# A chain of small attention steps set further apart beside a stream of matmuls, and three places for a convolution's input

## The chip, the cores and the metric

The kernel runs on one core of a Trainium2 chip. The metric is the device time of the whole program in microseconds (us); below, a time is the median of a few executions, and the profile is of one execution more. The engines are TensorE (PE, matmuls; PEld are its weight loads), VectorE (DVE), ScalarE (ACT), GpSimd (POOL) and SyncE (SP, which here only issues DMAs).

## The reference, cut to what matters

A transformer block of 512 tokens by 1024 features in float32: a feed-forward part, a hybrid mixer, a second feed-forward part, and then two more layers of other kinds. Only the mixer is touched by the change. It projects the normalized input `h` to many columns, and then runs two branches:

```python
proj = h @ w_in
# attention: 3 groups of 4 heads; group g has a causal window, dilation 1, 4, 16
q_a = partial_rope(q_a); k_a = partial_rope(k_a)      # rotates the first 32 of 128 dims
o_g, lse_g = dilated_window_attention(q_g, k_g, v_g)  # softmax over a near/far band
alpha = softmax(stack(lse_g)); att = sum(alpha * o_g)
# mLSTM: 4 heads of 256
qk = silu(causal_depthwise_conv(qk_m, conv_w, conv_b))   # 4 taps over time
hm = mlstm_chunkwise(q_m, k_m, v_m, i, log_f)
ml = sigmoid(o_m) * (rmsnorm(hm) * head_g)
y = (sigmoid(g_a) * (att @ w_att) + sigmoid(g_m) * (ml @ w_ml)) @ w_out
```

Each projection is computed as three products of split operands (high times high, low times high, high times low).

## The kernel before, in words

**Tiling.** Weights come in chunks, 128 output columns by 1024 input rows each. For a chunk `i` SyncE loads `RAW`; ScalarE writes the high half `WH` (`highs`, recorded at helper line 1031, event `hi`); VectorE writes the low half `WL` (`lows`, line 1651, event `lo`); TensorE runs 8 x 3 matmuls of 128x512 in `fm` (lines 410, 411, 413; the last one is line 415) into one of two side banks of PSUM; ScalarE evicts the bank (event `ev`). There are three slots of `WH` and `WL`, so `highs(i+2)` waits for the matmuls of chunk `i-1`.

**The side steps.** The small work of the mixer rides beside this stream. Each engine's program is written out by hand by its own function (`tensor_program`, `scalar_program`, `vector_program`), and in each the same generators stand in a list `behind.work`. `behind.step()` advances every generator of the list once, in the order in which they were appended. Each chunk has four steps. TensorE steps after every second `k`, so its steps lie 6, 12, 18 and 24 matmuls into the chunk. ScalarE and VectorE do all four steps of a chunk together. In their instruction order a chunk is:

```python
def fm():                      # scalar_program; vector_program has lows(i + 2)
    highs(i + 2)
    for _ in range(plan[i][1] // 2):
        behind.step()          # 4 times
    ...                        # then ScalarE waits for the matmuls of i and evicts (ev)
```

A generator that waits for a semaphore therefore holds up everything behind it in its engine's order, the next `highs` or `lows` among it. `behind.finish()` at the end of a turn runs what is left of the list with no matmuls between. `behind.bank()` hands out PSUM banks 5 and 6 for short use; all engines' programs must ask in the same order, so the yields of one generator are matched over the engines.

**The turns.** The mixer has eight turns `n`. Turns 0 to 3 project attention head `n` in nine chunks (q, k, v of three groups; `att_project`), turns 4 to 7 project mLSTM head `n-4` in eight chunks (four of them convolution inputs, then two values, then two gates; `ml_project`). Beside turn `n` run the small steps of the head of turn `n-1`: `attention(hd)` beside turns 1 to 4, `mlstm(hd)` beside turns 5 to 7 and what follows. Each is the first in the list of its turn. Behind them in the list come the generators of the chunks themselves, each appended after its chunk: `rope_first` (q and k: ScalarE issues two DMAs in its second step, VectorE rotates with three operations in its fifth), `to_tokens` (values: TensorE transposes, lines 585 and 586, ScalarE copies back), `conv` (VectorE's four operations in its first step, ScalarE's SiLU in its fourth).

**The chain of one attention head**, in the side steps of its turn (chunk `c` of a turn holds the steps 4c-3 to 4c):

| hand-over | engine, line | step before |
|---|---|---|
| scores near and far (`s near`, `s far`) | TensorE L612, L621 | 1 |
| mask and maxima (`mx near`, `mx far`) | VectorE L1660, L2002, L2008 | 3 |
| exponentials near and far (`ex near`, `ex far`) | ScalarE | 5 |
| `spread` | VectorE L1651 (32 columns) | 7 |
| `moved` (8 small matmuls) | TensorE L631 | 8 |
| `moved read`, `part in` | VectorE L1663, L1651 | 9 |
| `part` | ScalarE | 10 |
| `parts`, then far weights scaled (`pr far`) | VectorE L1651, L1657 | 11 |
| `back` (8 small matmuls) | TensorE L644 | 12 |
| near weights scaled (`pr near`) | VectorE | 13 |
| four rounds of transposes and products | TensorE L657, L667, ScalarE | 13 to 17 |

**The convolution's input** is one tile for each parity of the turn, `SETS[:, s, 8, :]`; ScalarE's eviction of the next one waits for the convolution that read the one before.

Of the kernel before, what the change touches and what calls it, by code (L numbers as in the profile page):

```python
# [16 lines left out]
T = 512  # L17
# [286 lines left out]
def small(m, name):  # L304
    a, b = SMALL[name]
    return m["SM"][:, a:b]
# [10 lines left out]

# [42 lines left out]
def tensor_program(pe, t, m):  # L363
# [215 lines left out]

    def to_tokens(i, dst, tok):  # L580
        b = yield from behind.bank()
        w.wait_ge(*at("ev", i))
        clear(b)
        for tb in range(3):
            pe.transpose(PS[:, b, tb * P:(tb + 1) * P], dst[:, tb * P:(tb + 1) * P], ident)
        pe.transpose(PS[:, b, 3 * P:4 * P], dst[:, 3 * P:4 * P], ident).then_inc(*tick("pe", "tt", i))
        free[b] = ("tok", i)
        behind.leave(b)
        tok.append(i)
# [12 lines left out]
    def attention(hd, s, tok):  # L602
        while len(tok) < 9:
            yield
        i0 = MIX + 1 + 9 * hd
        for g in range(3):
            w.wait_ge(*at("rope", i0 + 3 * g))
            w.wait_ge(*at("rope", i0 + 3 * g + 1))
# [15 lines left out]
        free[4] = free[7] = ("sm far", hd)  # L624
        for _ in range(7):
            yield
# [7 lines left out]
        free[b] = ("moved read", hd)  # L634
        yield
        behind.leave(b)
        for _ in range(3):
            yield
# [7 lines left out]
        ins.then_inc(*tick("pe", "back", hd))  # L646
        free[b] = ("back read", hd)
        yield
        behind.leave(b)
# [23 lines left out]
    def conv(i, tok):  # L673
        for _ in range(3):
            yield
        tok.append(i)
# [346 lines left out]
def scalar_program(a, t, m):  # L1023
# [202 lines left out]

    def to_tokens(i, dst, tok):
        b = yield from behind.bank()
        w.wait_ge(*at("tt", i))
        act(dst, PS[:, b, :], ACT.Copy, "tok", i)  # L1230
        behind.leave(b)
        tok.append(i)
# [27 lines left out]
    def attention(hd, s, tok):  # L1260
        while len(tok) < 9:
            yield
        near, far = small(m, "near"), small(m, "far")
        for _ in range(4):
            yield
# [5 lines left out]
        for n in range(4):  # L1271
            pr = weighed(m, 4 + n)
            act(pr, pr, ACT.Exp, *(("ex far", hd) if n == 3 else ()), bias=far[:, n:n + 1], accum_out=far[:, 4 + n:5 + n])
        for _ in range(3):
            yield
        b = yield from behind.bank()
        yield
        behind.leave(b)
        yield
        part = small(m, "part")  # L1280
        w.wait_ge(*at("part in", hd))
        act(part, part, ACT.Exp, "part", hd)
        yield
        yield
        b = yield from behind.bank()
        yield
# [15 lines left out]
    def conv(s, i, dst, tok):  # L1302
        for _ in range(3):
            yield
        w.wait_ge(*at("conv", i))
        act(dst, dst, ACT.Silu, "silu qk", i)
        tok.append(i)

    raw_free = [None, None]

    def ml_project(hd, s, tok):
        for c in range(4):
            i, b = fm(), side_bank()
            w.wait_ge(*at("mm", i))
            set_clear(s)
            if raw_free[s] is not None:
                w.wait_ge(*at("conv", raw_free[s]))
            raw_free[s] = i
            act(SETS[:, s, 8, :], PS[:, b, :], ACT.Copy, "ev", i)
            behind.work.append(conv(s, i, SETS[:, s, c, :], tok))  # L1320
# [322 lines left out]
def vector_program(v, t, m):  # L1643
# [324 lines left out]

    def to_tokens(i, dst, tok):
        b = yield from behind.bank()  # L1970
        behind.leave(b)
        tok.append(i)
# [14 lines left out]
    def attention(hd, s, tok):  # L1987
# [4 lines left out]
        PR, OF4 = m["PR"], C[:, C_OF4:C_OF4 + 4]  # L1992
        yield
        yield
        w.wait_ge(*at("s near", hd))
        w.wait_ge(*at("fm"))
        if hd > 0:
# [11 lines left out]
                        negate=True).then_inc(*tick("dve", "mx far", hd))  # L2009
        for _ in range(4):  # L2010
            yield
# [3 lines left out]
           OF4.unsqueeze(1).unsqueeze(1).to_broadcast([P, 4, 2, 4]), ALU.mult, "spread", hd)  # L2015
        yield
        b = yield from behind.bank()
        yield
        w.wait_ge(*at("moved", hd))
# [7 lines left out]
        tt(part[:, 4:8], lowest, far[:, 0:4], ALU.subtract, "part in", hd)  # L2027
        yield
        yield
        total_ = small(m, "sum")  # L2030
# [11 lines left out]
        for n in range(4):  # L2042
            pr = weighed(m, 4 + n)
            ts1(pr, pr, part[:, 4 + n:5 + n], ALU.mult, *(("pr far", hd) if n == 3 else ()))
        yield
        b = yield from behind.bank()
        yield
        back = small(m, "back")
# [18 lines left out]
    def conv(s, i, cc, raw, dst, tok):  # L2067
        wv = [vec(m, "conv_w", j * 16 + cc) for j in range(4)]
        w.wait_ge(*at("ev", i))
        done()  # L2070
        ts(dst, raw, wv[3], vec(m, "conv_b", cc), ALU.mult, ALU.add)
        for d in range(1, 4):
            done()
            stt(dst[:, d:T], raw[:, 0:T - d], wv[3 - d], dst[:, d:T], ALU.mult, ALU.add, *(("conv", i) if d == 3 else ()))
        for _ in range(3):
            yield
        tok.append(i)

    def ml_project(hd, s, tok):
        for which in range(2):  # L2080
            for c in range(2):
                behind.work.append(conv(s, side_fm()[0], which * 8 + hd * 2 + c, SETS[:, s, 8, :], SETS[:, s, 2 * which + c, :], tok))
        for c in range(2):
# [854 lines left out]
```

## Time and profile before

| | |
|---|---|
| time, median of 3 executions | 2733.23 us (2729.56 to 2739.18) |
| the profiled execution | 2731.48 us, its span 2729.7 us, mean granted TensorE clock 0.991 |
| TensorE matmuls busy | 2667.6 us, 98% of the span, 12626 instructions |
| VectorE busy | 1312.7 us, 48% |
| ScalarE busy | 920.8 us, 34% |
| GpSimd busy | 760.9 us, 28%, none after about 1710 us |
| the mixer's turns 1 to 7 | about 455 to 905 us of the span |

The span is the time from the first to the last instruction of the profiled execution. A share of busy time is an average; the matmuls' ends are modelled, so gaps between them are read from the waits and the timeline. The granted clock is the share of full speed (2.4 GHz) that TensorE was given; 0.50 is 1.2 GHz. A wait `A <- B` is idle time of A that ended when B's result came.

### The profile page before, as it was taken

The page shows a single profiled execution, that of the slowest core. Times are in us where ns is not written, and L with a number is a line of the kernel's source. Part 1 is how long each engine was busy: PE and PEld are TensorE (multiplying, and loading weights), DVE is VectorE, ACT ScalarE, POOL GpSimd, SP SyncE. Part 2 cuts the span into 40 slices and gives each one's busy share as a digit, 9 for nine tenths or more (in the row PEclk, how much of TensorE's full clock was granted, in tenths as well). Part 3 has the DMA queues.
Part 4 walks back from the last instruction along what each step waited for, and adds up shares of the span by engine and source line. Part 5 has one row for each costly group of instructions (what it writes and reads, how often), then busy time and mean ns, then how long its engine had stood idle before and what let it go on. Part 6 is the DMA issues. An engine that isn't in the chain of part 4 may idle for free.

```text
span 2729.7 us, 30564 instructions
## 1 busy us (share of the span) xinstructions
PE 2667.6 (98%) x12626; PEld 2171.8 (80%) x12626; DVE 1312.7 (48%) x1864; ACT 920.8 (34%) x1517; POOL 760.9 (28%) x628
## 2 busy tenths in 40 slices
PE   8999999999999999999999999999999999999999
PEld 7878887777777778887788666788888888888887
DVE  4344256566555544534525598463332554633323
ACT  4222234333344322422224344542222332422221
POOL 6563025574544568076600241000000000000000
PEclk9999999999999999999999999999999999999999
DMA  6543234443333354354433110123333323433332
GB/s 178 158 146 120 99 114 139 114 126 107 98 97 100 97 170 147 97 150 144 141 131 97 54 55 25 38 85 93 100 100 132 101 85 92 130 96 97 97 116 77
DMA packets 382379, 296.49 MB, mean 109 GB/s; under 512 B 15588, under 2 KB 335328, under 8 KB 382208
## 3 DMA queue, kind: packets, MB, share of 16 engines
q1 hardware_dynamic: 363632, 240.33, 29.4%
q0 software_dynamic: 17072, 52.64, 6.3%
q8 instruction: 99, 1.62, 0.2%
q10 hardware_dynamic: 1536, 1.58, 0.2%
q14 instruction: 40, 0.33, 0.0%
HBM read 290.79 MB, written 2.13 MB: 107 GB/s over the span
## 4 chain that ended last, share of the span: by engine, by line
PE 86%; DVE 9%; ACT 3%; POOL 1%; issue 1%; DMA 1%; SPq 0%; DVEq 0%; ACTq 0%; POOLq 0%
PE PS L410 18%; PE PS L411 17%; PE PS L413 15%; PE PS L490 7%; PE PS L488 7%; PE PS L489 7%; PE PS L415 2%; PE PS L447 1%; PE PS L448 1%; PE PS L449 1%; PE PS L940 1%; DVE SETS L1660 1%; DVE WL L1651 1%; PE PS L725 1%; PE PS L912 1%; DVE TS L1651 1%
## 5 line engine op out<-in xcount | busy, mean ns | idle before, releaser
L410 PE MATMUL PS<-HH,WH 128*128 128x512 f32 x2248 | 901.7, 401 | 0.1
L411 PE MATMUL PS<-HL,WH 128*128 128x512 f32 x2248 | 879.0, 391 | 0.0
L413 PE MATMUL PS<-HH,WL 128*128 128x512 f32 x1967 | 769.8, 391 | 0.0
L1651 DVE TENSOR_TENSOR WL<-RAW,WH 128x1024 fp32r<-128x1024 f32 (+1 forms) x306 | 404.1, 1323 | 551.2 <-ACT WH L1031 550.7
L410 PEld LDWEIGHTS PS<-HH,WH 128*128 128x128 f32 x2248 | 424.8, 189 | 111.6 <-issue 26.6
L411 PEld LDWEIGHTS PS<-HL,WH 128*128 128x128 f32 x2248 | 424.9, 189 | 89.8 <-issue 5.5
L1031 ACT ACTIVATE WH<-RAW 128x1024 fp32r<-128x1024 f32 (+1 forms) x318 | 330.2, 1040 | 360.4 <-PE PS L415 301.4
L413 PEld LDWEIGHTS PS<-HH,WL 128*128 128x128 f32 x1967 | 371.5, 189 | 79.3
L2505 POOL TENSOR_SCALAR ADA<-ADA,CA 128x512 f32<-128x512 f32 x168 | 297.5, 1771 | 9.9 <-DMA ADA<-in_ada_w 2.5
L2502 POOL TENSOR_TENSOR ASUM<-ASUM,ADA 128x512 f32<-128x512 f32 x168 | 229.9, 1368 | 14.0
L1651 DVE TENSOR_TENSOR WLr<-RAWD,WHr 128x1024 fp32r<-128x1024 f32 x82 | 101.4, 1237 | 259.1 <-ACT WHr L1031 259.1
L490 PE MATMUL PS<-WLr,UH 128*128 128x512 f32 x576 | 224.1, 389 | 0.0
L488 PE MATMUL PS<-WHr,UH 128*128 128x512 f32 x576 | 224.1, 389 | 0.0
L489 PE MATMUL PS<-WHr,UL 128*128 128x512 f32 x576 | 224.1, 389 | 0.0
L1651 DVE TENSOR_TENSOR TS<-TS,PS 128x512 f32<-128x512 f32 x112 | 76.9, 687 | 281.0 <-PE PS L415 277.7
L1031 ACT ACTIVATE UH<-TS 128x512 fp32r<-128x512 f32 x88 | 55.6, 632 | 399.2 <-DVE TS L1651 399.2
L1031 ACT ACTIVATE WHr<-RAWD 128x1024 fp32r<-128x1024 f32 x84 | 88.8, 1058 | 280.4 <-PE PS L490 260.3
L1031 ACT ACTIVATE TS<-PS 128x512 f32<-128x512 f32 (+2 forms) x177 | 100.2, 571 | 143.1 <-PE PS L657 44.7
L2513 POOL DMA_DIRECT2D ADA<-in_ada_w x192 | 112.7, 587 | 56.7 <-POOL ASUM L2502 44.9
L489 PEld LDWEIGHTS PS<-WHr,UL 128*128 128x128 f32 x576 | 108.1, 188 | 22.6
L488 PEld LDWEIGHTS PS<-WHr,UH 128*128 128x128 f32 x576 | 108.1, 188 | 22.3
L490 PEld LDWEIGHTS PS<-WLr,UH 128*128 128x128 f32 x576 | 108.1, 188 | 22.3
(358 smaller groups left out, 3278.8 us busy)
## 6 DMA issues: line engine op xcount, KB each, us to landing
ADA<-in_ada_w POOLq DMA_DIRECT2D x192, 256.0 KB, 3.1
RAW<-in_ffn_w_gate SPq DMA_DIRECT2D x88, 512.0 KB, 3.8
RAW<-in_ffn_w_up SPq DMA_DIRECT2D x88, 512.0 KB, 3.8
RAWD<-in_ffn_w_down SPq DMA_DIRECT2D x88, 512.0 KB, 3.5
RAW<-in_w_in SPq DMA_DIRECT2D x84, 512.0 KB, 3.8
RAW<-in_conv_w_in SPq DMA_DIRECT2D x24, 512.0 KB, 3.7
RAW<-in_attn_w_in SPq DMA_DIRECT2D x16, 512.0 KB, 3.8
RAW<-in_w_mlstm_branch SPq DMA_DIRECT2D x8, 512.0 KB, 4.5
```

The costliest lines, as they stand in the source:

```text
L410: pe.matmul(PS[:, b, :], wh[:, k, :], hi[:, k, :], start=k == 0, stop=False)
L411: pe.matmul(PS[:, b, :], wh[:, k, :], lo[:, k, :], start=False, stop=False)
L413: pe.matmul(PS[:, b, :], wl[:, k, :], hi[:, k, :], start=False, stop=False)
L415: pe.matmul(PS[:, b, :], wl[:, k, :], hi[:, k, :], start=False, stop=True).then_inc(*tick("pe", "mm", i))
L488: pe.matmul(PS[:, b, :], hi[:, k, ts], wh[:, j, :], start=k == 0, stop=False)
L489: pe.matmul(PS[:, b, :], lo[:, k, ts], wh[:, j, :], start=False, stop=False)
L490: ins = pe.matmul(PS[:, b, :], hi[:, k, ts], wl[:, j, :], start=False, stop=k == nk - 1)
L1031: return a.activation(out, of, func, **k).then_inc(*tick("act", *event))
L1651: return v.tensor_tensor(out, x, y, op).then_inc(*tick("dve", *event))
L2502: return g.tensor_tensor(out, x, y, op).then_inc(*tick("pool", *event))
L2505: return g.tensor_scalar(out, x, s1, None, op0).then_inc(*tick("pool", *event))
L2513: g.dma_start(ADA[:, i % 2, :], A["ada_w_2"][i // 96][k * P:(k + 1) * P, c * 512:(c + 1) * 512]).then_inc(*tick(f"ada{i % 2}", "ada in", i ...
```

## The change

It changes numbers of yields in the generators of the three engines, the tile that a convolution reads, and the wait that goes with it. The chain's steps become:

| hand-over | step before | step after |
|---|---|---|
| `s near`, `s far` (TensorE) | 1 | 3 |
| `mx near`, `mx far` (VectorE) | 3 | 5 |
| `ex near`, `ex far` (ScalarE) | 5 | 8 |
| `spread` (VectorE) | 7 | 10 |
| `moved` (TensorE) | 8 | 12 |
| `moved read`, `part in` (VectorE) | 9 | 14 |
| `part` (ScalarE) | 10 | 16 |
| `parts`, `pr far` (VectorE) | 11 | 17 |
| `back` (TensorE) | 12 | 19 |
| `pr near` (VectorE) | 13 | 21 |
| four rounds (TensorE) | 13 to 17 | 21 to 25 |

The core of the diff:

```diff
+def raw_tile(m, n):
+    return (m["SETS"][:, 0, 8, :], m["FG"][:, 0:T], m["FG"][:, T:2 * T])[n % 3]
 # all three programs
     def to_tokens(i, dst, tok):
+        yield
         b = yield from behind.bank()
 # tensor_program, attention
+        yield
+        yield
         for g in range(3):
             w.wait_ge(*at("rope", i0 + 3 * g))
...
-        for _ in range(7):
+        for _ in range(9):
             yield
         b = yield from behind.bank()
         w.wait_ge(*at("spread", hd))
...
+        yield
         behind.leave(b)
-        for _ in range(3):
+        for _ in range(5):
             yield
         b = yield from behind.bank()
         w.wait_ge(*at("parts", hd))
 # scalar_program, attention
-        for _ in range(4):
+        for _ in range(7):
             yield
         w.wait_ge(*at("mx near", hd))
 # vector_program, attention
-        yield
-        yield
+        for _ in range(4):
+            yield
         w.wait_ge(*at("s near", hd))
...
-        for _ in range(4):
+        for _ in range(5):
             yield
         w.wait_ge(*at("ex near", hd))
 # scalar_program, conv (the other two engines: 3 -> 5 too, before tok.append)
-        for _ in range(3):
+        for _ in range(5):
             yield
         w.wait_ge(*at("conv", i))
         act(dst, dst, ACT.Silu, "silu qk", i)
 # scalar_program, ml_project
-            if raw_free[s] is not None:
-                w.wait_ge(*at("conv", raw_free[s]))
-            raw_free[s] = i
-            act(SETS[:, s, 8, :], PS[:, b, :], ACT.Copy, "ev", i)
+            if len(raws) > 2:
+                w.wait_ge(*at("conv", raws[-3]))
+            act(raw_tile(m, len(raws)), PS[:, b, :], ACT.Copy, "ev", i)
+            raws.append(i)
```

No instruction that computes is added or taken away. In `attention` a borrowed bank is also held for two steps where it was held for one.

## Rows read from the trace of the kernel before

**Rows 1.** Waits of TensorE, 430 to 950 us: us in total, times, longest.

```profile
PE PS L644 <- DVE SM L1651: 9.9, 4, 3.5
PE PS L585 <- ACT SETS L1031: 7.8, 8, 3.1
PE PS L631 <- DVE SM L1651: 2.6, 1, 2.6
PE PS L612 <- DVE SETS L1651: 2.2, 1, 2.2
```

**Rows 2.** Windows: us, busy us and instructions by engine, clock, DMA, GB/s.

```profile
450.00:737.00 287.00, 268.58 (x1323) 218.84 (x1322) 169.91 (x237) 102.57 (x188) 166.41 (x133) 0.97 0.40 115
477.20:484.10 6.90, 6.66 (x24) 5.88 (x25) 6.69 (x14) 0.88 (x2) 6.10 (x6) 0.51 0.40 111
...
893.70:897.10 3.40, 3.26 (x10) 2.77 (x11) 3.37 (x5) 2.15 (x4) 2.97 (x4) 0.50 0.05 16
```

**Rows 3.** Timeline of VectorE, turn n=2: start us, us, line, tiles, [idle before].

```profile
528.25 1.23 DVE L1660 SCALAR_TENSOR_TENSOR PR<-PS,FMT 128x1024 f32<-128x1024 f32 x1 [1.01 <-PE PS L612]
...
531.89 1.22 DVE L2008 TENSOR_REDUCE SM<-PR 128x4 f32<-128x1024 f32 x1
535.73 1.23 DVE L1651 TENSOR_TENSOR WL<-RAW,WH 128x1024 fp32r<-128x1024 f32 x1 [2.61 <-ACT WH L1031]
537.58 0.19 DVE L1651 TENSOR_TENSOR SM<-SM,C 128x32 f32<-128x32 f32 x1 [0.63 <-ACT PR L1031]
...
543.04 0.68 DVE L1651 TENSOR_TENSOR TS<-TS,CS 32x512 f32<-32x512 f32 x1
...
544.35 0.68 DVE L1651 TENSOR_TENSOR SETS<-SETS,TS 32x512 f32<-32x512 f32 x1
...
545.62 0.23 DVE L1651 TENSOR_TENSOR SM<-SM 128x4 f32<-128x4 f32 x2
```

**Rows 4.** Timeline of ScalarE, the same turn.

```profile
537.45 0.50 ACT L1031 ACTIVATE PR<-PR,SM 128x256 f32<-128x256 f32 x1
...
539.59 0.60 ACT L1031 ACTIVATE SETS<-PS 128x512 f32<-128x512 f32 x1
540.08 1.05 ACT L1031 ACTIVATE WH<-RAW 128x1024 fp32r<-128x1024 f32 x1
```

**Rows 5.** Timeline of TensorE, the same turn: the last matmuls of two chunks.

```profile
533.72 0.39 PE L415 MATMUL PS<-HH,WL 128*128 128x512 f32 x1
...
539.16 0.39 PE L415 MATMUL PS<-HH,WL 128*128 128x512 f32 x1
```

**Rows 6.** VectorE by line and shape, 455 to 730: busy, mean ns, idle before.

```profile
L1651 DVE TENSOR_TENSOR WL<-RAW,WH 128x1024 fp32r<-128x1024 f32 x36 | 48.6, 1349 | 103.7 <-ACT WH L1031 103.7
L1651 DVE TENSOR_TENSOR SETS<-SETS,TS 32x512 f32<-32x512 f32 x18 | 16.5, 917 | 0.6
L1651 DVE TENSOR_TENSOR SETS<-SETS,CS 32x512 f32<-32x512 f32 x18 | 15.4, 858 | 0.0
L1651 DVE TENSOR_TENSOR TS<-TS,CS 32x512 f32<-32x512 f32 x18 | 15.3, 848 | 1.9
```

**Rows 7.** Timeline of VectorE and GpSimd around 608.8 us.

```profile
608.82 1.78 DVE L1651 TENSOR_TENSOR SETS<-SETS,CS 32x512 f32<-32x512 f32 x1
...
608.78 1.28 POOL L2502 TENSOR_TENSOR ASUM<-ASUM,ADA 128x512 f32<-128x512 f32 x1
```

**Rows 8.** Timeline of VectorE, turn n=4: a convolution's operations, and three of another.

```profile
669.14 0.78 DVE L1654 TENSOR_SCALAR SETS<-SETS,VT 128x512 f32<-128x512 f32 x1
669.96 3.57 DVE L1660 SCALAR_TENSOR_TENSOR SETS<-SETS,VT 128x511 f32<-128x511 f32 x3
...
691.04 2.32 DVE L1660 SCALAR_TENSOR_TENSOR SETS<-SETS,VT 128x511 f32<-128x511 f32 x3
```

**Rows 9.** Timeline of ScalarE and TensorE, turn n=7.

```profile
892.67 0.63 ACT L1031 ACTIVATE SETS<-SETS 128x512 f32<-128x512 f32 x1 [5.73 <-DVE SETS L1660]
...
893.84 0.90 PE L585 MATMUL PS<-C,SETS 128*128 128x128 f32 x3 [3.07 <-ACT SETS L1031]
```

More of the change, by code:

```diff
@@ L1227, in to_tokens @@
     def to_tokens(i, dst, tok):
+        yield
         b = yield from behind.bank()
@@ L1273, in attention @@
             act(pr, pr, ACT.Exp, *(("ex far", hd) if n == 3 else ()), bias=far[:, n:n + 1], accum_out=far[:, 4 + n:5 + n])
+        for _ in range(4):
+            yield
+        b = yield from behind.bank()
+        yield
+        yield
+        behind.leave(b)
+        yield
+        yield
+        part = small(m, "part")
+        w.wait_ge(*at("part in", hd))
+        act(part, part, ACT.Exp, "part", hd)
         for _ in range(3):
@@ L1277, in attention @@
         yield
-        behind.leave(b)
-        yield
-        part = small(m, "part")
-        w.wait_ge(*at("part in", hd))
-        act(part, part, ACT.Exp, "part", hd)
-        yield
-        yield
-        b = yield from behind.bank()
         yield
@@ L1302, in conv @@
     def conv(s, i, dst, tok):
-        for _ in range(3):
+        for _ in range(5):
             yield
@@ L1307, in conv @@
         tok.append(i)
-    raw_free = [None, None]
+    raws = []
     def ml_project(hd, s, tok):
@@ L1969, in to_tokens @@
     def to_tokens(i, dst, tok):
+        yield
         b = yield from behind.bank()
@@ L1992, in attention @@
         PR, OF4 = m["PR"], C[:, C_OF4:C_OF4 + 4]
-        yield
-        yield
+        for _ in range(4):
+            yield
         w.wait_ge(*at("s near", hd))
@@ L2009, in attention @@
                         negate=True).then_inc(*tick("dve", "mx far", hd))
-        for _ in range(4):
+        for _ in range(5):
             yield
@@ L2016, in attention @@
         yield
+        yield
         b = yield from behind.bank()
+        yield
         yield
@@ L2027, in attention @@
         tt(part[:, 4:8], lowest, far[:, 0:4], ALU.subtract, "part in", hd)
-        yield
-        yield
+        for _ in range(3):
+            yield
         total_ = small(m, "sum")
@@ L2045, in attention @@
         yield
+        yield
         b = yield from behind.bank()
+        yield
         yield
@@ L2074, in conv @@
             stt(dst[:, d:T], raw[:, 0:T - d], wv[3 - d], dst[:, d:T], ALU.mult, ALU.add, *(("conv", i) if d == 3 else ()))
-        for _ in range(3):
+        for _ in range(5):
             yield
@@ L2081, in ml_project @@
             for c in range(2):
-                behind.work.append(conv(s, side_fm()[0], which * 8 + hd * 2 + c, SETS[:, s, 8, :], SETS[:, s, 2 * which + c, :], tok))
+                behind.work.append(conv(s, side_fm()[0], which * 8 + hd * 2 + c, raw_tile(m, 4 * hd + 2 * which + c),
+                                        SETS[:, s, 2 * which + c, :], tok))
         for c in range(2):
```

## The prediction, made before the result was known

> **What bounds the kernel now.** The page first: TensorE is busy 98% of the span, so only what leaves TensorE idle, or slows its clock, can give time back. The mean granted clock is 0.991. Then the waits of TensorE over the mixer's turns [rows 1]: `back` (L644) waits 9.9 us in four heads, the value transposes (L585) 7.8 in eight, `moved` (L631) 2.6 once, the scores (L612) 2.2 once. Nothing else there reaches 1 us. Then the windows: at clock 0.97 over 287 us [rows 2], 17.2 us (287 x 0.03 x 2) lay at the lower level, 1.2 GHz. They are four dips, each right behind an idle stretch of 2.6 us or more: 6.9 us behind the first wait of L644 and 3.4 each behind others; a fifth of 3.4 follows the transposes' longest wait [rows 2, 9]. Half of a dip is lost: 8.6 and 1.7 us. Idle stretches of 2.2 us and less had no dip behind them. So the whole prize, waits and dips, is 9.9 + 2.6 + 2.2 + 5.0 (of the 7.8; the four transposes that run in `finish()`, about 0.7 each, keep theirs, since there a further yield has no matmuls behind it) + 8.6 + 1.7 = 30.0 us, 1.1%.
>
> **What the change moves.** No operation is added, so the cost is all in the order of the engines' queues. I go through it per hand-over, in the chunk in which each engine comes to it. What matters is that ScalarE and VectorE do a chunk's four steps in one go, behind `highs(i+2)` or `lows(i+2)`. Chunk 2 holds steps 5 to 8, chunk 3 holds 9 to 12.
>
> Before, VectorE scores in chunk 1 (step 3), and ScalarE's exponentials of chunk 2 (step 5) find the maxima ready. After, VectorE scores in step 5 and ScalarE takes the exponentials in step 8, which is the same chunk 2. **ScalarE now waits within chunk 2 for VectorE's work of chunk 2**, and behind it in its queue stand the eviction of chunk 2 and `highs` of chunk 3; behind that, on VectorE, stand `lows` of chunk 3, the rotation (step 9) and `spread` (step 10); and TensorE asks for `spread` in step 12, the end of chunk 3.
>
> With the rows of turn n=2, counted from the end of chunk 1's matmuls (533.72 + 0.39 = 534.11 [rows 5]):
> - VectorE's low half ends at 536.96, +2.85 [rows 3].
> - The four scoring operations run one behind the other from 528.25 to 533.11, 4.86 us [rows 3]: far maxima at +7.75.
> - The four far exponentials take 2.1 (537.45 to the next instruction at 539.59) [rows 4]: +9.85. The near ones, ready for at +5.4, are done by then.
> - Eviction and high half: 539.59 to 541.13, 1.55 [rows 4]: +11.4.
> - Low half, 1.23 [rows 3]: +12.65. Rotation of chunk 1's q, 543.04 to 545.03, 2.0 [rows 3]: +14.7. `spread` 0.19: **+14.9**.
> - TensorE is there at the end of chunk 3, two chunks of 5.44 on (533.72 to 539.16 [rows 5]): **+10.9**.
>
> So `moved` waits at least 4.0 us. That is without GpSimd in the way. VectorE's low half averages 1.35 here, and the three rotation operations 0.92 + 0.86 + 0.85 = 2.62 [rows 6]: two low halves and a rotation add 0.85. I take 4.9 us for turns 1 to 3. In turn 4 convolutions take the rotation's place: one behind the scores (step 5), one ahead of `spread` (step 9). Four operations take 4.4 us as at 669.14, and with 2.32 for three of them at 691.04 [rows 8] about 2.9 undisturbed. Scores +7.75, first convolution to +10.7 or +12.2, low half to +12.7 or +13.5, second one to +15.6 or +17.9, `spread` +0.2: a wait of 4.9 to 7.2, I take 6.0. Sum for L631: 3 x 4.9 + 6.0 = 20.7, against 2.6 before: **+18.1 us** (bounds: 3 x 4.0 + 4.9 = 16.9, or +14.3; above in the rival).
>
> **`back`** (L644, step 19, 18 matmuls or 4.1 us into chunk 5). VectorE comes to `parts` right behind the low half of chunk 5, at +2.85, and its chain to `parts` ended 0.8 us after the rotation (545.03 to 545.85 [rows 3]): +3.7 to 4.5 with GpSimd's share. `part in` (chunk 4) and ScalarE's `part` (step 16, the end of its chunk 4) come ahead of that, since TensorE's own wait at the end of chunk 3 gave them time. Left: 0 to 1 us a head, in turn 4 up to 2; I take 0.4 x 3 + 0.9 = 2.1. **-7.8 us** (bounds -9.9 and -4.9).
>
> **Scores** (L612): two steps more, 2.7 us, against a wait of 2.2: gone, **-2.2**.
>
> **mLSTM turns.** ScalarE's SiLU of the fourth convolution stood ahead of the eviction of chunk 5 and idled 5.73 us for VectorE; TensorE's transposes idled 3.07 behind it [rows 9]. After, the SiLU is one chunk later, no eviction waits for the convolution just before it (three tiles), and the transposes have 1.36 us more. VectorE's own work of the chunk ends before. The 5.0 us go, with the dip's 1.7: **-6.7** (bounds -3 and -6.7: the lesser if only the 1.36 us count). SyncE's and GpSimd's queues are passed by nothing that blocks them: the loads wait for `lo` of four chunks before, and the low half of chunk 3, 5 us late at +12.65, is wanted by TensorE only in chunk 5 of the turn, at about +22.
>
> **Dips.** Four waits of 5 us instead of mostly 3: each again has a dip behind it, some two, but part of it may lie within the wait itself. I take 7.1 us lost instead of 8.6: **-1.5** (bounds -5 for dips half within the waits, +5 for two behind each).
>
> **Sum:** 18.1 - 7.8 - 2.2 - 6.7 - 1.5 = -0.1. From the profiled execution's 2731.48 us (its span 2729.7 and 1.8 around it) that is 2731.4. The median of the runs shown, 2733.23, lies 1.75 above the profiled one, so I put the median at 2733; the times below are on that footing.
>
> **A rule of the Trainium skill.** Row first: the rotation's middle operation took 1.78 us at 608.82, beside a GpSimd operation from 608.78 to 610.06 [rows 7]; its mean is 0.86 [rows 6]. The scoring operations took 1.22 and 1.23 in the same stretch [rows 3]. The Trainium skill, "SBUF — State Buffer", Who interferes with whom, says that VectorE and GpSimd share one port pair as an exclusive lock, which a VectorE operation with both inputs in SBUF contends for against GpSimd's reads. By that rule, the trace agrees, and every link that I put behind ScalarE's late high half is of that kind; the sum above has it only as an average.
>
> **The rivals.**
> - *Slower: GpSimd stretches the new path.* The new path to `spread` has five operations with both inputs in SBUF behind the scores (low half, three of the rotation, `spread`). Each that meets GpSimd costs up to 1.1 us (1.78 against 0.67 [rows 7]). All five: 9.5 us a wait. It decides from the point at which the four waits of L631 sum to 29 us (7.2 each, three hits a turn), where the total is +8.2. With 3.5 us more a wait and second dips (+5 in place of -1.5) the total is +20.4: 2754. For it: GpSimd is busy 166 of 287 us [rows 2]. Against: the mean of 36 low halves is only 0.12 over the clean one [rows 6].
> - *Faster: the wait at `moved` is short or absent*, if ScalarE isn't held up in chunk 2 as I read the order. Then the whole prize of 30 us comes: 2703. Against: the position of step 8 in chunk 2, and `highs(i+2)` ahead of each chunk's steps. The existing wait of L631 in turn 4 speaks for my reading: there `spread` stood behind one convolution, and 2.6 us were lost. A half-way case has each term at its low bound, no GpSimd in the way: 14.3 - 9.9 - 2.2 - 6.7 - 5 = -9.5, or 2724.
> - *The wait only moves* (my forecast): `back` is freed, `moved` is late. Within it, if the mLSTM's part gives only 3, the sum is +3.6: 2737.
> - *Nothing happens*, since the steps are fewer than the turn has (25 of 36 or 32), isn't a rival of its own: the chain moves in any case.
>
> **How the numbers follow.** My forecast case 0.62, the half-way faster case 0.13, the full gain 0.09, slower by contention 0.16. A measurement of this kernel can tell about 0.3%, 8.2 us, from no change. Of the forecast case all is within 0.3%, save 0.02 at the slower end. Faster by over 0.3% is 0.13 + 0.09 = 0.22, slower 0.16 + 0.02 = 0.18, within 0.60. The range reaches from 2717, below the half-way case, to 2747, into the slower one: it leaves out the full gain and about half of the slower case. The forecast case alone spans 2725 to 2742.
>
> **What the changed profile would show.** L631 waits of 4 to 7 us in all four heads, ended by VectorE's 128x32 product; L644 under 1 us each; L612 and the transposes after 700 us gone; ScalarE idle inside chunk 2 for VectorE's maxima, and the low half of chunk 3 about 12 us behind chunk 1's end, not 8. Dips remain behind L631. I am wrong if L631 hardly waits, or if a wait shows up at L657 or L667 (then a later round is the late one), or if the convolutions' turns have a new wait.

## The result, and the profile after

The changed kernel takes 2743.6 us (median of 8), the kernel before in the same comparison 2735.8: a ratio of 1.0037, 95% interval 1.0025 to 1.0048. It is **slower by 0.37%, about 10 us** (the two medians by themselves lie 7.8 us apart). The profiled execution has a span of 2740.3 us against 2729.7 before, with a mean granted clock of 0.987 against 0.991. Line numbers are shifted by the new lines: `moved` (L631 before) is L639, `back` (L644) L653, the value transposes (L585) L591, the flush of the modulation L393.

TensorE's waits over the mixer, in the kernel after (engine, line, what it waited for: us in total, times, longest), answer [rows 1]:

```profile
PE PS L639 <- DVE SM L1665: 23.3, 4, 8.1
PE PS L591 <- ACT SETS L1041: 2.7, 4, 0.7
PE PS L653 <- DVE SM L1665: 2.1, 1, 2.1
PE PS L591 <- DVE SM L1677: 1.3, 1, 1.3
PE PS L393 <- DVE SM L1665: 1.2, 1, 1.2
```

`moved` waited 2.6 us once; now it waits in all four heads, 23.3 us. `back` fell from 9.9 to 2.1 us, the scores' 2.2 are gone, and the transposes keep only the four waits of 0.7 us at the turns' ends. Two waits are new: the transposes and the flush, for VectorE's reads of small tiles. A wait of 0.9 us at the ones-product behind turn 7 (L744 before) is gone. In all 23.4 us became 30.6.

The windows of the kernel after (us, busy us and instructions of TensorE, its weight loads, VectorE, ScalarE, GpSimd, then granted clock) answer [rows 2]:

```profile
449.00:736.00 287.00, 256.21 (x1270) 210.89 (x1269) 155.75 (x222) 95.90 (x178) 149.78 (x122) 0.95 0.40 109
476.90:483.70 6.80, 4.27 (x18) 3.39 (x19) 6.59 (x10) 0.00 (x0) 4.92 (x5) 0.50 0.71 201
753.40:756.80 3.40, 3.40 (x6) 1.70 (x6) 1.71 (x5) 0.00 (x0) 2.60 (x3) 0.50 0.21 57
736.00:950.00 214.00, 214.00 (x933) 162.84 (x932) 124.69 (x190) 90.14 (x126) 108.88 (x91) 0.97 0.36 100
```

Over the 287 us of the attention's turns the clock is 0.95, where it was 0.97: five dips, 30.7 us in sum at 1.2 GHz, against four and 17.1. The dip of 6.8 us at 476.9 began while TensorE still waited at `moved` (it was busy 4.27 of the 6.8). In the mLSTM turns TensorE now has no idle time at all (214.0 of 214.0), yet four dips of 3.4 us, one in each of the three turns and one behind; the second row from below is the first.

The same turn n=2 whose rows the prediction used, in the kernel after: TensorE's last matmul of chunk 3 and `moved`, then ScalarE, then VectorE (start us, us, line, operation, tiles, [idle before]).

```profile
544.72 0.39 PE L420 MATMUL PS<-HH,WL 128*128 128x512 f32 x1
548.90 0.30 PE L639 MATMUL PS<-SM,C 128*32 128x8 f32 x8 [3.79 <-DVE SM L1665]
```

```profile
539.49 0.40 ACT L1041 ACTIVATE PR<-PR,SM 128x128 f32<-128x128 f32 x1 [3.68 <-DVE SM L2017]
...
541.88 0.51 ACT L1041 ACTIVATE PR<-PR,SM 128x256 f32<-128x256 f32 x1 [0.41 <-DVE SM L2023]
...
543.87 0.58 ACT L1041 ACTIVATE SETS<-PS 128x512 f32<-128x512 f32 x1
544.34 1.04 ACT L1041 ACTIVATE WH<-RAW 128x1024 fp32r<-128x1024 f32 x1
```

```profile
540.62 1.22 DVE L2023 TENSOR_REDUCE SM<-PR 128x4 f32<-128x1024 f32 x1
545.42 1.22 DVE L1665 TENSOR_TENSOR WL<-RAW,WH 128x1024 fp32r<-128x1024 f32 x1 [3.58 <-ACT WH L1041]
546.75 0.68 DVE L1665 TENSOR_TENSOR TS<-TS,CS 32x512 f32<-32x512 f32 x1
...
548.06 0.68 DVE L1665 TENSOR_TENSOR SETS<-SETS,TS 32x512 f32<-32x512 f32 x1
548.67 0.17 DVE L1665 TENSOR_TENSOR SM<-SM,C 128x32 f32<-128x32 f32 x1
```

Chunk 1's matmuls ended at 534.23. ScalarE idles 3.68 us for VectorE's near maxima (first line). The far ones are ready at 541.84, +7.61; ScalarE idles 0.41 us more for them, runs four exponentials, evicts, and writes the high half of chunk 3 until 545.38, +11.15. VectorE, idle 3.58 us meanwhile, writes the low half, rotates, and writes `spread` until 548.84, **+14.61** (14.9 in the prediction). TensorE had been there since 545.11, +10.88: it idles 3.79 us.

From the end of turn 0 to the end of turn 7 the two profiled executions took 458.5 and 468.0 us, turn by turn: 68.4, 65.4, 68.9, 67.4, 60.3, 62.1, 66.0 before, and 71.7, 74.5, 71.0, 66.7, 61.5, 61.3, 61.2 after. Turns 1 to 3 lose 14.5 us, turns 4 to 7 win 5.0. Past the mixer the chunks of the two executions stay 9 to 11 us apart to the end, so that the loss is the mixer's.

One stretch far behind the mixer, 1500 to 1900 us, has the same code in every version of this document, and still its profiles differ: TensorE was at 1.2 GHz there for 23.9 us in the kernel before and in the one after, and for 20 to 38 us over all versions. At half the speed that is a difference of up to 9 us in code that no edit touches.

### The profile page after: what moved, and what is told of

Its sections match the earlier page's. It is cut to its first block, busy times and chain, and to the rows that moved or that the text cites. A ratio compares the mean times of both kernels' runs of the same rounds, so it can differ in the third digit from the quotient of the medians.

```text
span 2740.3 us, 30556 instructions
## 1 busy us (share of the span) xinstructions
PE 2669.9 (97%) x12622; PEld 2174.7 (79%) x12626; DVE 1306.6 (48%) x1864; ACT 922.7 (34%) x1517; POOL 758.8 (28%) x628
## 4 chain that ended last, share of the span: by engine, by line
PE 88%; DVE 7%; ACT 2%; POOL 1%; issue 1%; DMA 1%; another core or an unknown queue 0%; SPq 0%; DVEq 0%; ACTq 0%; POOLq 0%
PE PS L415 18%; PE PS L416 18%; PE PS L418 16%; PE PS L495 7%; PE PS L494 7%; PE PS L493 7%; PE PS L420 2%; PE PS L452 1%; PE PS L453 1%; PE PS L454 1%; PE PS L950 1%; PE PS L735 1%; PE PS L922 1%; DVE WL L1665 1%; DVE TS L1665 1%
```

## The experiments

Theories: **A**, ScalarE is held within chunk 2 by VectorE's work of the same chunk, and the next high half stands behind it; the two halves of the change add up. **C**, VectorE's own load and its contention with GpSimd make `spread` late. Further ones are named where they come up.

### The second half alone

The kernel before, with `raw_tile`, the SiLU two steps later and the value transposes one step behind:

```diff
+        yield                                   # to_tokens, three engines
-            act(SETS[:, s, 8, :], PS[:, b, :], ACT.Copy, "ev", i)
+            act(raw_tile(m, len(raws)), PS[:, b, :], ACT.Copy, "ev", i)
```

> The kernel before with the second half of the change alone: three places for the convolution's input, SiLU two steps later, value transposes one step behind; the attention chain as before. Theory A (each half does what its rows say, and the halves add up): the transposes' waits after 700 us, 5.0 us, and their dip go; the waits of `back` (9.9), `moved` (2.6) and the scores (2.2) stay. Time 4 to 8 us under the kernel before. Theory B (the mLSTM turns only hand their gain to the clock: the small matmuls of the denominator have a dip in each turn once the waits are gone): dips behind L715 and L725 in three or four of the turns instead of two, and a time within 3 us of the kernel before.

Measured: 2726.5 us, ratio 0.9965 (0.9953 to 0.9977), 10 us faster, more than Theory A's 4 to 8. TensorE's waits of this kernel:

```profile
PE PS L650 <- DVE SM L1658: 6.8, 3, 3.5
PE PS L591 <- ACT SETS L1037: 2.8, 4, 0.7
PE PS L637 <- DVE SM L1658: 2.8, 1, 2.8
PE PS L618 <- DVE SETS L1658: 2.1, 1, 2.1
```

The first three lines are `back`, the transposes and `moved`, the fourth the scores. The transposes keep 2.8 of 7.8 us: all 5.0 of the mLSTM turns are gone, as the prediction has it. But three dips of 3.4 us stand behind 720 us as before, now all at the denominator's small matmuls (turns 6, 7 and behind), so the clock gave nothing back there: Theory B is right on the dips and wrong on the time. `back` also lost its wait of turn 4, 3.1 us, in which VectorE's chain to `parts` stood behind a convolution; the three others are as before.

### The first half alone

The kernel after, with the second half taken back:

```diff
-            act(raw_tile(m, len(raws)), PS[:, b, :], ACT.Copy, "ev", i)
+            act(SETS[:, s, 8, :], PS[:, b, :], ACT.Copy, "ev", i)
-        yield                                   # to_tokens, three engines
```

> The kernel after with the convolution's and the transposes' half taken back; the attention chain two to five steps apart stays. Theory A: the `moved` waits of about 23 us stay, so does the wait of the transposes in the mLSTM turns (5 us); time 12 to 18 us over the kernel before. Theory B (the halves disturb each other, for instance in turn 4, where convolutions and the chain meet): the `moved` wait of turn 4 falls from 8.1 us to about 5, and the time is within 5 us of the kernel after.

Measured: 2748.5 us, ratio 1.0047 (1.0031 to 1.0064), 13 us slower.

```profile
PE PS L638 <- DVE SM L1663: 25.4, 4, 10.1
PE PS L590 <- ACT SETS L1040: 6.9, 7, 3.1
PE PS L590 <- DVE SM L1663: 3.3, 1, 3.3
```

`moved` waits 25.4 us, up to 10.1 in turn 4, so that Theory B, by which that wait falls to 5, is out. There ScalarE's eviction of chunk 2 stands behind the SiLU of the first convolution, which waits for VectorE, and VectorE then idles 2.1 us for the high half. The chain's half is the loss, as Theory A has it, and the convolution's half a gain that it hides. By the ratios +13 and -10 leave +3, where the whole measured +10; the intervals (0.12% and 0.17%) nearly span the gap of 7 us. TensorE's waits do add up: -8.0 and +15.1 us for the halves, +7.2 for the whole. The time at 1.2 GHz in the mixer does not: 27 us before, 27 and 38 with the halves, 44 with both. So if the halves hinder each other, it is by way of the clock; one profile of each doesn't show more. One thing varies between profiled executions with the same code in turn 2: this kernel took 68.4 us there without a wait at `back`, the kernel after 74.5 with one of 2.1 and 10.2 us of dips.

### ScalarE's exponentials in the next chunk

```diff
 # scalar_program, attention
-        for _ in range(7):
+        for _ in range(8):
             yield
         w.wait_ge(*at("mx near", hd))
...
-        for _ in range(4):
+        for _ in range(3):
             yield
```

> The kernel after with ScalarE's exponentials one step later, step 9 for step 8, so that they stand in chunk 3, behind the eviction of chunk 2 and the high half of chunk 3; nothing else moves. Theory A (`moved` waits because ScalarE is held within chunk 2 by VectorE's maxima of the same chunk, and the high half stands behind it): the low half of chunk 3 ends about 8.3 us behind chunk 1's end instead of 12.7, `spread` lies at 10.5 to 12, and the four `moved` waits fall from 23.3 us to 0 to 5; time 20 to 28 us under the kernel after. Theory C (VectorE's own load, rotation and GpSimd's share, makes `spread` late whatever ScalarE does): the waits stay above 15 us in sum.

Measured: 2723.6 us, ratio 0.9954 (0.9940 to 0.9969): one step on one engine turns 10 us of loss into 12 to 13 us of gain. Waits, and VectorE in the same turn n=2, in this kernel:

```profile
PE PS L639 <- DVE SM L1665: 12.1, 3, 8.1
...
PE PS L591 <- DVE SM L1677: 1.3, 1, 1.3
```

```profile
536.27 1.22 DVE L2023 TENSOR_REDUCE SM<-PR 128x4 f32<-128x1024 f32 x1
537.41 1.21 DVE L1665 TENSOR_TENSOR WL<-RAW,WH 128x1024 fp32r<-128x1024 f32 x1
...
540.65 0.17 DVE L1665 TENSOR_TENSOR SM<-SM,C 128x32 f32<-128x32 f32 x1
```

The low half of chunk 3 follows the maxima without a pause (it ended at 538.62, 1.13 us behind them; it was 4.8 in the kernel after), and TensorE doesn't wait at `moved` in this turn. Turns 1 and 3 keep 2.4 and 1.6 us. Theory A holds for turns 1 to 3: of 15.2 us 11 are gone. **In turn 4 it fails**: the wait stays at 8.1 us whatever ScalarE does. There Theory C is right: scores and two convolutions stand on VectorE ahead of `spread`.

### GpSimd taken off the port

The kernel after; in sums 5 to 15 of the modulation all steps but the first compute on one element instead of 128x512, so that the modulation is not the reference's. GpSimd is busy 54 us of the 287 of the attention's turns, for 150:

```diff
-                    ts1(src, src, CA[:, k:k + 1], ALU.mult)
-                    w.wait_ge(*here("pool"))
-                    tt(ASUM[:, :], ASUM[:, :], src, ALU.add, "ada step", i)
+                    ...                       # 5 <= a < 16; the two operations stay for the others
+                    ts1(ASUM[0:1, 0:1], src[0:1, 0:1], CA[0:1, k:k + 1], ALU.mult, "ada step", i)
```

> The kernel after, with GpSimd's sums of the modulation left out from the sixth to the sixteenth (its loads stay, of its arithmetic one element a step): it hardly touches the port that it shares with VectorE in the mixer. The modulation that comes out of it is not the reference's. Theory A (held ScalarE is the base, contention is the rest): the `moved` waits fall from 23.3 us to 3 x 4.0 + 5 = 17, each close to the 4.0 worked out from undisturbed rows (4.9 in turn 4), and the `back` wait of 2.1 us in turn 2 goes. Theory C (contention is most of it): they fall below 8 us in sum.

It ran once: 2734.2 us, its span 2732.4 us against 2740.3 in the kernel after.

```profile
PE PS L639 <- DVE SM L1665: 16.0, 4, 4.6
PE PS L591 <- ACT SETS L1041: 2.8, 4, 0.7
PE PS L393 <- DVE SM L1665: 1.3, 1, 1.3
```

The four waits of `moved` were 3.8, 3.8, 3.8 and 4.6 us: the floor that the undisturbed rows gave (4.0 and 4.9). So of 23.3 us 16.0 are the order of the queues and 7.3 are GpSimd's contention with VectorE, 3.5 of them in turn 4. (The four waits of the kernel after, 6.0, 3.8, 5.5 and 8.1 us, came again within 0.2 us in the version with the value transposes at once, below.) Turn 2 has the same 3.8 us in both: there GpSimd does nothing while VectorE goes from the scores to `spread`. `back` no longer waits: its 2.1 us were contention as well. The kernel after shows that in VectorE's chain to `parts`, 2.9 us in these lines, 0.9 in [rows 3]:

```profile
562.33 1.52 DVE L1665 TENSOR_TENSOR SM<-SM 128x4 f32<-128x4 f32 x3
563.88 0.18 DVE L1680 RECIPROCAL SM<-SM 128x4 f32<-128x4 f32 x1
564.10 1.15 DVE L1665 TENSOR_TENSOR SM<-SM 128x4 f32<-128x4 f32 x2
```

The flush's wait of 1.3 us stays; it is not GpSimd's. The transposes' wait of turn 2 is gone, but for another reason: this profile has a dip of 10.2 us there, for 3.4, and TensorE itself comes later.

### VectorE's scores in the chunk before

The other way to part the two engines; the exponentials stay in step 8.

```diff
 # vector_program, attention
-        for _ in range(4):
+        for _ in range(3):
             yield
         w.wait_ge(*at("s near", hd))
...
-        for _ in range(5):
+        for _ in range(6):
             yield
         w.wait_ge(*at("ex near", hd))
```

> The kernel after with VectorE's scoring one step earlier, step 4 for step 5, so that it stands in chunk 1; ScalarE's exponentials stay in step 8, `spread` in step 10. A second way of taking VectorE's maxima and ScalarE's exponentials out of one chunk. Theory A: as with the exponentials one step later, the `moved` waits of turns 1 to 3 fall from 15.2 us to 0 to 5 in sum; VectorE idles in chunk 1 until TensorE's scores of step 3, which costs nothing. In turn 4 the two convolutions no longer have the scores ahead of them in chunk 2, so that its wait falls too, from 8.1 to about 3 us (it stayed at 8.1 with the exponentials one step later). Theory C: the waits follow VectorE's load alone, and stay as they were with the later exponentials, 2.5, 0 and 1.8 us and 8 in turn 4.

Measured: 2717.8 us, ratio 0.9941 (0.9926 to 0.9957).

```profile
PE PS L639 <- DVE SM L1665: 6.6, 3, 3.5
...
PE PS L653 <- DVE SM L1665: 2.1, 1, 2.1
```

`moved` waits 1.4, 1.6 and 3.5 us (turns 1, 3 and 4). Turn 4's wait fell from 8.1 to 3.5, since the scores no longer stand in the chunk of the first convolution. So Theory A's forecast came true (0 to 5 us in turns 1 to 3, about 3 in turn 4); what is left in turn 4 is VectorE's own load, as C has it.

### The value transposes at once

The kernel after without the `yield` in `to_tokens`, convolution and chain as they are.

> The kernel after with the value transposes back in the first step behind their chunk; chain and convolution stay. Theory D (the transposes one step behind meet the bank that `moved` holds: in turn 2 they take it in step 14, right after TensorE has left it, and wait for VectorE's `moved read`): that wait of 1.3 us goes, and turn 2 gets 1 to 6 us shorter; the flush's wait of 1.2 us in turn 1 stays. The transposes of the mLSTM turns don't wait even so, since their evictions come in time with three input places: their extra step was not needed. Theory E (it was needed): 0.6 to 1.1 us of wait come back in each of four mLSTM turns, and the time is 2 to 4 us over the kernel after.

Measured: 2742.4 us, ratio 1.0025 (1.0011 to 1.0038), not told apart from the kernel after by the intervals. The wait for VectorE's small read went from turn 2 (1.3 us) and came up in turn 4 (1.2 us), and one transposes' wait of 0.8 us came back in turn 7. So neither D nor E: by TensorE's waits (31.9 us for 30.6) this part of the change is worth about 1 us, by the times it can't be told. The new wait itself is one for a borrowed bank, as these lines of the kernel after show:

```profile
552.93 0.16 DVE L1665 TENSOR_TENSOR MOD<-PS,VT 128x4 f32<-128x4 f32 x1 [2.95 <-PE PS L394]
...
554.51 0.98 DVE L1665 TENSOR_TENSOR SETS<-SETS,TS 32x512 f32<-32x512 f32 x1
555.42 0.14 DVE L1677 COPY SM<-PS 128x8 f32<-128x8 f32 x1
```

```profile
555.71 0.52 PE L591 MATMUL PS<-C,SETS 128*128 128x128 f32 x3 [1.32 <-DVE SM L1677]
```

In turn 2 the transposes take over the bank which `moved` had, in the step in which TensorE leaves it; they wait until VectorE has copied it out at 555.42 to 555.56. The copy stands behind two other things in VectorE's chunk: the read of the flush, for which VectorE idled 2.95 us, and the three rotation operations. It is not late because of `moved`: with the exponentials in step 9 `moved` doesn't wait in this turn, and the transposes wait the same 1.3 us. The wait of the flush in turn 1 is of the same kind: it takes the bank of `back`, and the read of that one stands behind VectorE's low half of chunk 6.

### The denominator's small matmuls in two steps

The version with the exponentials in step 9, and one `yield` within the mLSTM's one-column matmuls, matched on the other engines. The trace has 20 of them in a row for each head, 2.3 us long; the 80 of the text below are those of four heads. The edit also turns their order round, so that 8 come before the `yield` and 12 behind it.

```diff
-        for tb in range(4):
+        for tb in (3, 2, 1, 0):
+            if tb == 2:
+                yield
             for sb in range(tb + 1):
```

> The kernel with the exponentials in step 9, and in addition the mLSTM's denominator (L715 of the kernel before, 80 matmuls of one column) split over two steps, six full matmuls between the halves. Theory F (the dips of the mLSTM turns come from this stretch of small matmuls, which has no waits in it): of the three dips of 3.4 us that stood there one or none is left, and the time falls by another 3 to 5 us. Theory G (they are left over from waits elsewhere): they stay, and the time is that of the exponentials in step 9 within 2 us.

Measured: 2733.3 us, ratio 1.0002 (0.9988 to 1.0017), 13 us slower than without the split.

```profile
PE PS L639 <- DVE SM L1668: 12.0, 3, 8.0
PE PS L756 <- DVE TS L1674: 8.3, 4, 3.8
```

The dips went from three to none in turns 5 to 7 (one is left behind turn 7, with a wait of 3.8 us before it), as Theory F has it. One profile of each doesn't settle the cause, though: two versions have none in these turns without any split, the one with the scores in step 4 and a later one below. But the split pushed the next steps on by one: VectorE's `mdg` came into chunk 4, and the ones-product asks for it in the same chunk. L756 waits 8.3 us, and turns 5 to 7 take 61.9, 61.7 and 60.7 us, no less than 61.5, 61.3 and 61.2. In the profiled executions 15 us lie between the two versions: under 2 of them come before 930 us, 6 between 930 and 960 us, at the last chain's wait of 3.8 us and its dip, and 8 between 1580 and 1770 us, in code that is the same in both, where dips made up 38 us at the lower level against 20. How often that stage falls so, the profiles don't say; the twelve executions of this version reach from 2723.9 to 2740.0 us.

### `moved` six steps later

On the version with the exponentials in step 9:

```diff
 # tensor_program, attention: moved in step 18, back in step 23
         for _ in range(9):
             yield
+        w.wait_ge(*at("sm far", hd))
+        for _ in range(6):
+            yield
         b = yield from behind.bank()
         w.wait_ge(*at("spread", hd))
...
-        for _ in range(5):
+        for _ in range(3):
             yield
         b = yield from behind.bank()
         w.wait_ge(*at("parts", hd))
```

The other two engines' steps move along. The added wait for VectorE's mask (`sm far`) never held TensorE up in the profile.

> The kernel with the exponentials in step 9, and TensorE's `moved` in step 18 instead of 12 (`part in` and `part` in step 20, `parts` in 21, `back` in 23, the rounds in 25 to 29). Theory A (what is left at `moved` after the step-9 version, 12.1 us with 8.1 in turn 4, is VectorE's load in chunks 2 and 3, two convolutions beside the scores in turn 4, and six steps or 8 us more cover it): the waits of `moved` fall to 0 to 1 us in sum, `back` may wait up to 1 us a head since `parts` is again in the chunk before; time 10 to 16 us under the step-9 version. Rival: the last rounds reach into the end of turn 4, and what is gained at `moved` comes back as waits in its last chunks, or in a first wait of turn 5.

Measured: 2710.7 us, ratio 0.9917 (0.9902 to 0.9932).

```profile
PE PS L591 <- ACT SETS L1044: 7.4, 5, 4.7
...
PE PS L397 <- DVE SM L1666: 0.9, 1, 0.9
...
PE PS L656 <- DVE SM L1666: 0.2, 1, 0.2
```

`moved` waits nowhere, and turns 1 to 3 take 62.2, 63.4 and 63.6 us, against 71.7, 74.5 and 71.0 in the kernel after. The rival came true in one place: in turn 4 the transposes wait 4.7 us for an eviction. ScalarE shows why:

```profile
681.62 0.21 ACT L1044 ACTIVATE SM<-SM 128x8 f32<-128x8 f32 x1 [2.68 <-DVE SM L1666]
681.73 0.58 ACT L1044 ACTIVATE SETS<-PS 128x512 f32<-128x512 f32 x1
```

It idled 2.68 us for VectorE's `part in`, in the same chunk, and the eviction stood behind it. It is the mechanism of `moved` once more.

### `part` one step later, and then the split again

```diff
 # scalar_program, attention
+        yield
         part = small(m, "part")
         w.wait_ge(*at("part in", hd))
         act(part, part, ACT.Exp, "part", hd)
-        for _ in range(3):
+        for _ in range(2):
             yield
```

> The kernel with `moved` in step 18, and ScalarE's `part` one step later, in step 21 for 20, the first of chunk 6. In the step-18 version the one long wait left was that of turn 4: the value transposes waited 4.7 us for the eviction of chunk 5, which stood on ScalarE behind `part`, which waited for VectorE's `part in`, and that behind a convolution of the same chunk. Theory A (again two engines' work in one chunk, the later one holding the first's queue): that wait goes with its dips, turn 4 takes 61 to 63 us instead of 66.8, `back` waits 0 to 1 us more; time 3 to 7 us under the step-18 version. Rival: the wait only moves to `back` (step 23 of the same chunk), which then waits 3 to 5 us in turn 4.

Measured: 2713.2 us, ratio 0.9923 (0.9910 to 0.9936): not told apart from the version before it (0.9917), so the forecast gain of 3 to 7 us did not show in the time.

```profile
PE PS L656 <- DVE SM L1667: 3.6, 2, 3.4
PE PS L591 <- ACT SETS L1044: 3.3, 5, 0.7
```

In the profile the 4.7 us are gone and turn 4 takes 63.4 us, while `back` (first line) now waits 3.4 us in it: both the theory and the rival came out in part. This profile has no dips in the mLSTM turns, without any split. It is, though, that of the fastest of six executions (2708.1 us), and the profile of the version before that of its slowest (2719.5).

The second version adds the split, and two steps ahead of the ones-product:

```diff
 # tensor_program, mlstm (the other two engines' steps move along)
-        yield
-        yield
+        for _ in range(4):
+            yield
         b = yield from behind.bank()
         w.wait_ge(*at("mdg", hd))
```

> The version with `part` in step 21, and the mLSTM's denominator split over two steps as before, but now with the ones-product behind it (L744 of the kernel before) two steps later, so that it isn't asked for in the chunk in which VectorE makes its input. Theory F (the dips of the mLSTM turns come from the stretch of small matmuls; the split took them away, and its gain went into the 8.3 us of waits of L744): no dip of 3.4 us in turns 5 to 7 and behind, L744 waits 0 to 1 us, and the time is 2 to 6 us under the version without the split if that one shows three or four such dips, and the same within 2 us if it shows none.

Measured: 2708.4 us, ratio 0.9902 (0.9888 to 0.9916), the fastest of all: **27 us under the kernel before and, by the two ratios, 37 under the changed one**. Its windows, the attention's turns and the mLSTM's:

```profile
450.00:706.00 256.00, 248.42 (x1263) 205.10 (x1263) 158.34 (x221) 95.05 (x179) 156.77 (x126) 0.99 0.44 121
706.00:930.00 224.00, 221.44 (x994) 170.76 (x993) 133.62 (x203) 96.37 (x134) 116.90 (x99) 1.00 0.36 103
```

The mLSTM turns have clock 1.00, one wait of 1.6 us at the ones-product and one of 1.0 at the transposes. Against the version without the split the intervals overlap (0.9910 to 0.9936 and 0.9888 to 0.9916), and the profiles speak against a gain: in the mixer this version is 3 us longer than the one without the split, and it gets ahead only between 1560 and 1760 us, by 8 us, in code that is the same in both. Theory F's "the same within 2 us if it shows none" is not contradicted, and no gain of the split is shown.

## Why the prediction was right and wrong, point by point

The forecast was a sum of -0.1 us, no change that can be told; the measured one is +10, still within the range, but not its middle. The path was read rightly; what failed are four terms of the sum: the dips behind the waits (forecast -1.5, measured +2.6), the dips of the mLSTM turns (-1.7, measured +1.7), the size of the wait at `moved` (20.7, measured 23.3), and the borrowed bank, which the sum put at nothing (2.5).

- **The order of the queues: right.** ScalarE held in chunk 2, the late low half of chunk 3, `spread` at +14.9 (measured +14.61), 4.0 us of wait undisturbed (3.8 three times with GpSimd light). The two one-step experiments confirm for turns 1 to 3 that it is the shared chunk.
- **`moved`, 20.7 us: 23.3.** Turns 1 to 3 gave 15.2 for 14.7; turn 4 gave 8.1 where 6.0 was taken and 7.2 was the bound. There the convolutions took 4.6 and 4.1 us, near their bound of 4.4, and `spread` itself 1.25 for 0.19, which no row of before had shown so long. Mis-sized by 2.6 us.
- **`back`, 2.1 us left: 2.1**, but the sum was met by luck: it came in one turn, by GpSimd's contention, where each head was to have under 1 us. **Scores, transposes: right**, 2.2 and 5.0 us gone.
- **The borrowed bank: missed, 2.5 us.** The section on the change tells that a bank is now held two steps; the prediction didn't price it. TensorE's next borrower waits for VectorE's read of the bank, and that read stands behind VectorE's other work of the chunk: 1.3 us in turn 2, 1.2 at the flush of turn 1. Both stay where `moved` waits less or not at all. Against it, 0.9 us at the ones-product went, which the prediction had not counted either.
- **Dips behind `moved`: -1.5 forecast.** TensorE was busy in 22.0 of the 30.7 us at the lower level, half of it lost, 11.0, against 8.4 before (16.8 us): +2.6. Part of each dip did lie within the wait, as taken, but three dips were 6.8 us long, and `back` in turn 2 had another 6.8 behind it. Off by 4.1 us. Their length did not follow from that of the wait; the term's bounds (-5 to +5) held.
- **Dips in the mLSTM turns: the wrong step.** The prediction took the fifth dip away with the wait before it, -1.7. Two dips of the profile before (801.5 and 862.9) were never followed to their cause: they began 0.1 to 1 us after the last of the denominator's 20 small matmuls had started, with no wait before them, and after the change each mLSTM turn and the last chain had one. From 10.2 to 13.7 us, +1.7 for -1.7. Over the ten versions with the matmuls in one step, 23 of 40 such stretches had a dip at their end, from none of four to all four; of the eight split ones none had. So the place is shown, that a split keeps them away is likely (it gained no time that can be told), and what brings a dip about in a given turn stays open.
- The terms so corrected add up to -0.1 + 2.6 + 2.5 - 0.9 + 4.1 + 3.4 = +11.6 us, where the two spans lie 10.6 apart; the 1 us too many is not assigned (half of a dip may be too much where small matmuls fill it: the eight of `moved` took 0.30 us in a dip and 0.25 outside one).
- **The rivals.** "GpSimd stretches the new path" was the slower one, with 29 us at `moved` as its point; 23.3 were reached. The slower result came from four smaller terms of one sign (`moved`, the bank, the dips behind waits and those at the small matmuls); of the rival only its contention and its second dips took part. The case slower had a chance of 0.18.

The Trainium skill, "SBUF — State Buffer", Who interferes with whom, was drawn on for the port that VectorE and GpSimd share. The runs agree with it: with most of GpSimd's arithmetic left out the waits of `moved` fell by 7.3 us to 16.0, where the undisturbed rows gave 16.9. That it is a port which the two engines share, no run here can tell. One reading of the prediction is off beside it: the scoring operations of 1.22 and 1.23 us are of turn 2, 80 us ahead of the rotation that it compares them with.

## What to carry to other kernels

Count a hand-over in the units in which each engine's queue really advances. Here two engines do four steps at one point, so three more steps put consumer and producer into the same chunk, and everything behind the consumer in its queue (here the next weights' high half) became late; one step more on the one engine, or one less on the other, was worth over 20 us. When a chain is stretched, look at what it holds while it is stretched, banks above all, and look for clock dips behind stretches of small matmuls as well as behind waits; how long a dip will be could not be told here from either.

## What the runs showed of the hardware that was not expected

- TensorE's clock fell to 1.2 GHz for 3.4 us with no idle time before it or in it: in the kernel after at 753.4, at the end of 20 one-column matmuls (751.20 to 753.49) and while the wider ones behind them ran (busy 3.40 of 3.40 us). It did so in all four heads there, and in none of the four in the `part`-later version, whose code is the same at this place.
- GpSimd's element operations beside VectorE's stretched an operation on 32 columns from 0.17 to 1.25 us (697.44 in turn 4 of the kernel after, beside GpSimd's addition from 697.14 to 698.64), and small 4-column ones (562.33 above: three took 1.52 us, and 0.43 with GpSimd light).
- Waits of the same 3.8 us had dips of different lengths behind them: 3.4 us in the kernel after, 6.8, 10.2 and 6.8 in the one with GpSimd light. The flush's wait of 1.3 us had a dip of 3.4 us behind it in that one (496.3) and none in the kernel after, so that the prediction's "2.2 us and less had no dip" held for the kernel before alone. What the clock adds to a wait is not fixed by its length.
